# The first differential head: its mask and maximum ahead of two low parts of weights, three low parts behind the next softmax steps

## What is computed

```
q, k, v = jnp.split(h @ w_in, 3, axis=-1)
q = rope_partial(q.reshape(B, T, H, 2, dh), cos, sin) * (dh ** -0.5)
k = rope_partial(k.reshape(B, T, H, 2, dh), cos, sin)
...
for i in range(T // Q_BLOCK):                       # 4 blocks of 128 queries
    L = (i + 1) * Q_BLOCK
    s = einsum('bhiqd,bhikd->bhiqk', q[block i], k[:L])
    p = softmax(where(mask, s, -inf), axis=-1)
    a = p[:, :, 0] - lam * p[:, :, 1]
    outs.append(einsum('bhqk,bhkv->bhqv', a, v[:L]))
```

## Time and profile before

| | before |
|---|---|
| median of 3 runs | 1542.72 us (1540.8 to 1542.75) |
| the profiled execution | 1540.82 us |
| its span, first to last instruction | 1539.5 us |
| PE busy | 1513.5 us, 98% of the span |
| DVE busy | 985.3 us, 64% |
| ACT busy | 660.6 us, 43% |
| POOL busy | 163.9 us, 11% |

### The profile page before, as it was taken

One profiled execution on the slowest core, in us unless ns is written; L12 is line 12 of the kernel. 1 busy time (PEld: TensorE's weight loads), 2 busy tenths in 40 slices (PEclk: granted clock), 3 DMA queues, 4 the chain that ended last, 5 costly groups with the idle time before them and its releaser, 6 DMA issues.

```text
span 1539.5 us, 18851 instructions
## 1 busy us (share of the span) xinstructions
PE 1513.5 (98%) x7498; PEld 1235.9 (80%) x7498; DVE 985.3 (64%) x1592; ACT 660.6 (43%) x1118; POOL 163.9 (11%) x153
## 2 busy tenths in 40 slices
PE   8999999999999999999999999999999999999998
PEld 6778878888888888777777878888888876888776
DVE  7567667866666664777776743434344539989764
ACT  6445434513233233455565532413233436555660
POOL 0000002000000002111111100000000102675200
PEclk9999999999999999999999999999999999999999
DMA  9344444566656553122212243333333222212131
GB/s 370 120 129 148 140 137 161 167 215 192 194 189 200 185 162 98 55 69 69 69 56 83 96 117 96 96 96 96 98 94 102 72 87 68 70 53 75 37 109 55
DMA packets 52458, 181.82 MB, mean 118 GB/s; under 512 B 5793, under 2 KB 6689, under 8 KB 52370
## 3 DMA queue, kind: packets, MB, share of 16 engines
q1 hardware_dynamic: 52370, 180.61, 37.4%
HBM read 177.05 MB, written 3.41 MB: 117 GB/s over the span
## 4 chain that ended last, share of the span: by engine, by line
PE 90%; DVE 4%; ACT 2%; POOL 2%; DMA 1%; issue 1%; SPq 0%; DVEq 0%; ACTq 0%
PE PS L520 24%; PE PS L523 23%; PE PS L521 23%; PE PS L530 2%; PE PS L531 2%; PE PS L533 2%; PE PS L576 2%; PE PS L912 1%; PE PS L757 1%; PE PS L776 1%; PE PS L595 1%; PE PS L1067 1%; POOL sb_TMD L2345 1%; PE PS L1061 1%; PE PS L1062 1%; DMA sb_rg<-ada 1%
## 5 line engine op out<-in xcount | busy, mean ns | idle before, releaser
L520 PE MATMUL PS<-sb_Hh,sb_Wh 128*128 128x512 f32 (+1 forms) x1016 | 404.8, 398 | 2.8 <-DVE sb_Hl L1708 2.8
L523 PE MATMUL PS<-sb_Hh,sb_Wl 128*128 128x512 f32 (+1 forms) x1016 | 396.0, 390 | 0.6 <-DVE sb_Wl L1677 0.6
L521 PE MATMUL PS<-sb_Hl,sb_Wh 128*128 128x512 f32 (+1 forms) x1016 | 396.0, 390 | 0.0
L1111 ACT ACTIVATE sb_Wh<-sb_RAW 128x1024 fp32r<-128x1024 f32 (+1 forms) x218 | 228.3, 1048 | 289.9 <-PE PS L523 283.0
L1677 DVE TENSOR_TENSOR sb_Wl<-sb_RAW,sb_Wh 128x1024 fp32r<-128x1024 f32 (+1 forms) x218 | 268.1, 1230 | 83.7 <-ACT sb_Wh L1111 83.6
L520 PEld LDWEIGHTS PS<-sb_Hh,sb_Wh 128*128 128x128 f32 (+1 forms) x1016 | 189.6, 187 | 59.6 <-issue 16.0
L520 PE MATMUL PS<-sb_Oh,sb_Wh 128*128 128x512 f32 x600 | 235.2, 392 | 0.4 <-ACT sb_rg L1295 0.4
L523 PE MATMUL PS<-sb_Oh,sb_Wl 128*128 128x512 f32 x600 | 233.7, 389 | 0.0
L521 PE MATMUL PS<-sb_Ol,sb_Wh 128*128 128x512 f32 x600 | 233.5, 389 | 0.0
L523 PEld LDWEIGHTS PS<-sb_Hh,sb_Wl 128*128 128x128 f32 (+1 forms) x1016 | 189.6, 187 | 42.9 <-DVE sb_Wl L1677 1.1
L521 PEld LDWEIGHTS PS<-sb_Hl,sb_Wh 128*128 128x128 f32 (+1 forms) x1016 | 189.8, 187 | 39.9 <-issue 1.2
(11 more groups left out here) (376 smaller groups left out, 2041.1 us busy)
## 6 DMA issues: line engine op xcount, KB each, us to landing
sb_RAW<-w SPq DMA_DIRECT2D x128, 512.0 KB, 3.6
sb_ARW<-ada SPq DMA_DIRECT2D x86, 512.0 KB, 4.5
sb_RAW<-diff_in SPq DMA_DIRECT2D x24, 512.0 KB, 3.7
sb_RAW<-gla_in SPq DMA_DIRECT2D x20, 512.0 KB, 3.7
sb_RAW<-in_b SPq DMA_DIRECT2D x16, 512.0 KB, 3.8
sb_RAW<-gla_wo SPq DMA_DIRECT2D x8, 512.0 KB, 3.6
sb_RAW<-diff_wo SPq DMA_DIRECT2D x8, 512.0 KB, 3.6
sb_RAW<-wo SPq DMA_DIRECT2D x8, 512.0 KB, 3.7
```

The costliest lines, as they stand in the source:

```text
L520: mm(to[0:m, :], WH[si][:, k, 0:m], hi[:, k, :], start=first, stop=False)
L521: mm(to[0:m, :], WH[si][:, k, 0:m], lo[:, k, :], start=False, stop=False)
L523: ins = mm(to[0:m, :], WL[si][:, k, 0:m], hi[:, k, :], start=False, stop=last)
L1111: act(WH[slot_of(b)][:, :, 0:m], RAWS[raw_of(b)][:, 0:8 * m].rearrange("p (k m) -> p k m", k=8), ACT.Copy).then_inc(*done("w_hi", b))
```

## The change

Only the order of DVE's instructions around tick 3 and tick 4 of the differential layer is written anew.

```
             for n in range(3):
                 diff_tick(n)
-            for n in range(3):
-                w_next(DIFF + n)
-            for n in range(3, 23):
+            diff_max(0, 3)
+            w_next(DIFF)
+            diff_combine(0, 3)
+            diff_tick(4)
+            w_next(DIFF + 1)
+            w_next(DIFF + 3)
+            w_next(DIFF + 4)
+            for n in range(5, 23):
                 diff_tick(n)
                 if n < 22:
                     w_next(DIFF + n)
```

## The result

| | before | changed |
|---|---|---|
| median of 6 runs | 1542.60 us (1540.80 to 1544.87) | 1550.81 us (1550.07 to 1553.01) |
| profiled execution | 1540.82 us | 1551.20 us |
| its span | 1539.5 us | 1549.9 us |

The ratio is 1.0055, with a 95% interval from 1.0043 to 1.0066: the changed kernel is slower by 8.2 us in the medians. The forecast was 1550.0.

A forecast was written before the change was run, and what follows sets the result against it. PE, busy for 98% of the span, was taken as the bound. Stalls less waits, 2.44 - 0.86 + 6.47 - 1.56 = 6.49 us, plus 1.7 for the clock made 8.2: forecast 1550.0 us, range 1546.5 to 1553.5.

The forecast's parts named there:

- first stall: PE's third matmul of block 4 waits for DVE's low part, now behind mask and maximum of i = 3: 2.44 us.
- turn of i = 3: PE's turning of i = 3's weights: its 0.86 us wait goes, so it comes 1.58 us later than before.
- third matmul of block 5: PE waits there 6.47 us for DVE's low part, behind tick 4; with the earlier 1.58 it is 8.05 later.
- stalls less waits, clock held: Sum on PE up to block 6 without clock loss: 2.44 - 0.86 + 6.47 - 1.56 = 6.49 us.
- start of block 6: PE's block 6 begins 6.49 us later than before, 8.2 with the 1.7 us of lost clock.
- The clock, second stall: PE's clock falls to 1.2 GHz in the wait at block 5, costing 1.7 us, bounds 0 and 2.6.
- The clock, first stall: PE's clock does not fall in the 2.4 us wait at block 4, so no loss there.
- A: Rival: both PE stalls but no loss of clock, 1547.3 to 1549.2 us; chance 0.22.
- B: Rival: not slower; block 5's low part is ready when PE comes, only waits go, 1538.4 to 1540.3 us; chance 0.05.
- the 2.42 of the waits: PE's waits at the turns before the change, 0.86 + 1.56 = 2.42 us: all there is to gain.
- C: Rival: PE's later waits shrink by as much as the stall at block 5, about 1541 to 1543 us; chance 0.05.
- D: Rival: late low parts hold up loads, block 8 or 9 late too, from 1553.5 us up; chance 0.06.

The follow-up runs named there:

- both filled: Changed kernel with 8 small matmuls put on PE in the wait at block 4 and 25 at block 5: 1547.69 against 1541.28 us, 6.4 over before.
- low 5 back: Changed kernel with block 5's low part right behind block 4's: 1543.55 against 1542.38 us; with 8 small matmuls in the wait at block 4, 1542.79 against 1541.28.
- the last experiment: Changed kernel with block 4's low part ahead of the i = 3 mask, block 5's between its maximum and combine: 1541.04 against 1542.38 us, ratio 0.9990.
- low part 5 between: Changed kernel with block 5's low part moved between tick 4's maxima and combines: 1548.29 us, 6.2 over before.

## Why the prediction was right, and where it was not

The range held the time and the sign was right, by the steps that were written down. That the first difference of the medians is the 8.2 us of the sum to the tenth is luck: the stretch grew by 9.3 and 10.6 us in the two profiles, and the clock's part was sized too small. Counted from the scores of i = 3 (636.67 before, 637.64 after):

| step | said | profile after |
|---|---|---|
| scores' start to mask | 1.17 us | 638.82 - 637.64 = 1.18 |
| mask to the low part of block 4 | 1.61 | 640.43 - 638.82 = 1.61 |
| first stall, third matmul of block 4 later by | 2.44 | 4.06 - 1.62 = 2.44 |
| turn of i = 3 later by | 1.58 | 9.19 - 7.50 = 1.69 |
| mask of i = 2 to the low part of block 5 | 5.63 | 654.19 - 648.54 = 5.65 |
| third matmul of block 5 later by | 8.05 | 17.82 - 9.69 = 8.13 |
| stalls less waits, clock held | 6.49 | 6.67 in the stretch, both filled |
| clock | 1.7 (0 to 2.6) | 2.6 in this profile, 4.0 in the next |
| start of block 6 later by | 8.2 | 26.73 - 17.47 = 9.26 |

**The stalls.** Right to 0.1 us each. The 0.2 that the sum lacks is the step behind a wait: it is 0.34 us (641.70 to the next matmul at 642.04 in the same timeline), not 0.228, once for each stall.

**The clock, second stall.** Mechanism right, size too small: the low clock lasted 5.7 us of matmuls, the upper bound taken from the start of the span, and cost 2.6, not 1.7. The step that was mis-sized is "I take 1.7, since the four matmuls between look even". Its source was weak as well: in the profile before, the granted clock is 1.00 where those matmuls are slow, and it stays there in the windows up to 12 us:

```profile
0.00:3.00 3.00, 1.96 (x9) 1.97 (x10) 0.17 (x1) 1.28 (x1) 0.19 (x4) 1.00 0.18 42
3.00:5.00 2.00, 2.00 (x10) 1.77 (x10) 0.00 (x0) 0.00 (x0) 0.00 (x0) 1.00 1.01 377
```

So no row shows the low clock at the start of the span; what a fall costs is shown by the windows and steps behind the two stalls.

The Trainium skill (TensorE: Matmul & The Clock Gate, Part 1: The HAM clock gate) gives 426.7 ns from start to start at the low clock; the trace agrees, 656.48 - 656.05 = 0.43.

**The clock, first stall.** Wrong: "and not within the first, 2.4 us". Five profiled executions had this stall unfilled; in four of them the clock fell in it, for a loss of 1.6 us (33.17 - 31.58, and 26.96 - 25.39). I had read the 3.9 us at the end of the span as how long idleness has to last; it is only how long it lasted once.

**The two errors and the forecast.** Had the clock in the second stall been sized right, the sum would be 9.1 on the profiled execution, which showed 9.27 in the stretch; the rest of its 10.4 us (1551.20 - 1540.82) is the 0.97 ahead of the change and 0.1 elsewhere. In the medians the cost is 8.2 and 9.0. Why the medians show 8.2 and 9.0 where the stretches show 9.3 and 10.6 was not shown. The scatter of the rest of the kernel is large enough for it, and it is not mainly the clock's: in one set of 23 executions of the kernel before, five had a mean granted clock of 1.000, and both the fastest of the set, 1539.91 us, and the slowest, 1545.04, are among them.

**The rivals.** A, no lost clock, describes the filled kernel: 6.4 over before. B was priced wrongly: with the low part of block 5 ready and that of block 4 late, the first stall of 2.44 us stays and eats up the 2.42 of the waits. That is the kernel "low 5 back", 1.2 and 1.5 over before. To win the waits, both low parts must be in time, which is the last experiment, 1.3 under before. C, that the second stall is given back, did not occur; its price for the first stall alone, nothing, holds to 0.1 us up to the start of block 6 and to 0.5 in the stretch. D did not occur: from 630 to 860 us, which holds blocks 8 and 9 and all those behind them in this layer, the view of PE's waits in the changed kernel has the two stalls and nothing else. The chances that go into "slower" (0.62, 0.22 and 0.06) add up to 0.90, not 0.91.

## What to carry to other kernels

When one engine is the bound, ask of each piece of work on another engine not how long it takes but who needs it first: here a reduction was put ahead of a subtraction that the bound engine needed 0.6 us after it began its next block, and a second subtraction behind work that itself waits for that engine. Such a circle (PE waits for DVE's low part, which stands behind a step that waits for PE's scores) cost the whole round trip here, 6.3 us, though DVE stood idle for 2.9 us in it. An idle gap of DVE, seen in its own row as a wait for PE, is where such work belongs. A stall of PE of some microseconds can be dearer than its length: where the clock fell, it took 1.6 us in addition behind a stall of 2.3 us, and 2.6 behind one of 6.3.

## What the runs showed of the hardware

The clock fell in the first stall, after idleness of 2.3 us, in four of five profiled executions. It fell in each of the three unfilled second stalls of 6.3 us, and not in the one stall of 2.80 us. In two profiles it also fell after much less. Far from the change all eleven profiled executions have one wait of PE in a stretch of small matmuls; in the last experiment it is 1.17 us, and the windows there read:

```profile
1252.00:1255.00 3.00, 1.84 (x12) 1.02 (x11) 1.33 (x3) 2.59 (x5) 0.00 (x0) 1.00 0.72 272
1255.00:1256.00 1.00, 0.98 (x3) 0.61 (x4) 0.83 (x2) 0.76 (x3) 0.00 (x0) 0.94 0.69 66
1256.00:1259.00 3.00, 3.00 (x8) 2.34 (x7) 2.19 (x3) 1.08 (x2) 0.00 (x0) 0.50 0.38 153
```

PE is busy there but for 1.2 us, and the clock is at 0.50 for some 3.4 us. It fell only after PE had gone on at 1255.02. The other such fall is that of the kernel with low part 5 between, where the wait is 1.25 us. In the nine other profiles this wait is 0.75 to 1.06 us (0.94 in the kernel before, at 1255.45), and the clock stays at 1.00. So the two longest waits are the two with a fall; that their length decides is not shown. In the profile with the wait of 1.25 us, nine matmul steps took 1266.82 - 1263.18 = 3.64 us where 9 x 0.228 = 2.05 would do, a loss of 1.6 us.

The kernel before itself ran between 1539.91 and 1545.04 us in 23 executions on one chip. Both of these executions had a mean granted clock of 1.000; even at 0.9995 an execution of this length would lose only 0.8 us by the clock, so most of the 5.1 us between them is something else. What it is stays open.
